# A two-layer diffusion backbone on eight cores: two tiles of the mixing normed ahead, six PSUM banks for its first tile, and a rearranged opening

## The reference

```
for l in range(DEPTH):
    mx = silu(c) @ w_mod[l] + b_mod[l]           # 9 vectors: shift, scale, gate for 3 sub-layers
    h  = h + 0.5 * mx[2] * swiglu(norm_modulate(h, norm_ffn1, mx[0], mx[1]), w_ffn1_in, w_ffn1_out)
    n  = norm_modulate(h, norm_mix, mx[3], mx[4])
    u, q, k, v = split(n @ w_in)                 # 512, 512, 128, 128 columns
    h  = h + mx[5] * concat(pool_mixer(u) @ w_pool * pool_scale, attention(rope(q), rope(k), v)) @ w_out
    h  = h + 0.5 * mx[8] * swiglu(norm_modulate(h, norm_ffn2, mx[6], mx[7]), w_ffn2_in, w_ffn2_out)
return rmsnorm(h, norm_final)
# norm_modulate(x) = x * rsqrt(mean(x^2) + eps) * gain * (1 + scale) + shift;  swiglu: (silu(a) * b) @ w_out
```

## Time and profile before

| | us |
|---|---|
| median of 3 runs | 2917.92 (2917.41 to 2920.98) |
| profiled execution | 2925.55, span 2924.0 on its slowest core (core 0) |
| spans of the 8 cores | 2909.7 to 2924.0, mean granted clock 0.976 to 0.978 |
| busy: PE, DVE, ACT, POOL | 91%, 30%, 27%, 13% |

### The profile page before, as it was taken

The page is one execution under the profiler, slowest core; times in us unless marked ns, Lnnn a source line. Parts: engine busy times, 40 slices in busy tenths (PEclk is TensorE's granted clock), DMA queues, the critical chain, the costliest instruction groups (busy, mean ns, idle before and its releaser), DMA issues.

```text
span 2924.0 us, 46537 instructions; the slowest of 8 cores (2909.7 to 2924.0 us)
## 1 busy us (share of the span) xinstructions
PE 2666.2 (91%) x16692; PEld 1406.1 (48%) x16976; DVE 866.4 (30%) x1568; ACT 798.4 (27%) x1276; POOL 389.3 (13%) x572
## 2 busy tenths in 40 slices
PE   3899999997888799999899999999977888999998
PEld 1455555553444355555455555555534444444445
DVE  2211221214555511132123222222134553112224
ACT  3211321112454511132123112311125453122122
POOL 2111001002322211101100000000023221000000
PEclk9899999998999899999999999999989999999999
DMA  9466356352000165545644341344520003434453
GB/s 212 78 101 107 53 98 103 73 103 48 8 12 6 28 117 97 92 82 87 109 77 79 61 78 32 71 71 78 94 57 8 14 1 66 73 63 88 79 96 130
DMA packets 75706, 214.42 MB, mean 73 GB/s; under 512 B 9184, under 2 KB 17120, under 8 KB 74976
## 3 DMA queue, kind: packets, MB, share of 16 engines
q0 software_dynamic: 60896, 187.33, 37.8%
q1 hardware_dynamic: 14592, 24.12, 2.6%
HBM read 390.32 MB, written 8.39 MB: 136 GB/s over the span
## 4 chain that ended last, share of the span: by engine, by line
PE 85%; issue 4%; DVE 4%; ACT 3%; DMA 3%; POOL 1%; SPq 0%; DVEq 0%; ACTq 0%; POOLq 0%
PE ps L125 74%; PE ps L123 11%; DMA arena<-wab 2%; ACT arena L761 1%; DVE arena L459 1%; ACT arena L468 1%; DMA arena<-gains 1%; DVE arena L663 1%; POOL arena L418 0%; DVE arena L513 0%; SPq L143 0%; DVE arena L788 0%; DVE arena L684 0%; ACT arena L661 0%; ACT arena L429 0%
## 5 line engine op out<-in xcount | busy, mean ns | idle before, releaser
L125 PE MATMUL ps<-arena 128*128 128x512 bf16 (+8 forms) x14581 | 2511.2, 316 | 200.2 <-ACT arena L761 45.6
L125 PEld LDWEIGHTS ps<-arena 128*128 128x128 bf16 (+1 forms) x14829 | 1242.4, 98 | 1290.1 <-issue 274.1
L123 PE MATMUL ps<-arena 128*128 128x512 bf16 (+6 forms) x2111 | 657.0, 335 | 50.8 <-ACT arena L415 26.8
L565 DVE TENSOR_TENSOR arena<-arena,ps 128x512 bf16<-128x512 f32 (+2 forms) x484 | 291.9, 603 | 1184.4 <-PE ps L123 1128.9
L563 ACT ACTIVATE arena<-ps 128x512 f32<-128x512 f32 (+2 forms) x484 | 256.1, 529 | 1183.4 <-PE ps L123 1178.2
L513 DVE SCALAR_TENSOR_TENSOR arena<-ps,arena 128x512 f32<-128x512 f32 (+3 forms) x296 | 177.1, 609 | 569.5 <-PE ps L123 569.3
L123 PEld LDWEIGHTS ps<-arena 128*128 128x128 bf16 (+1 forms) x2147 | 207.2, 99 | 220.9 <-issue 85.6
L468 ACT ACTIVATE arena<-arena 128x512 bf16<-128x512 f32 (+3 forms) x256 | 179.6, 725 | 275.6 <-DVE arena L459 192.8
L143 POOL DMA_DIRECT2D arena<-wab x176 | 94.0, 538 | 645.3 <-PE ps L123 643.5
L761 ACT ACTIVATE arena<-ps 128x1024 bf16<-128x1024 f32 x167 | 161.7, 1027 | 53.3 <-PE ps L123 49.1
L459 DVE TENSOR_TENSOR arena<-arena 128x512 f32<-128x512 f32 (+3 forms) x256 | 156.2, 631 | 26.4 <-ACT arena L431 15.1
(11 more groups left out here) (34 smaller groups left out, 196.2 us busy)
## 6 DMA issues: line engine op xcount, KB each, us to landing
arena<-wab POOLq DMA_DIRECT2D x176, 512.0 KB, 6.5
arena<-wo POOLq DMA_DIRECT2D x64, 704.0 KB, 7.8
arena<-wmod POOLq DMA_DIRECT2D x144, 256.0 KB, 6.5
outT<-arena SPq DMA_DIRECT2D x26, 256.0 KB, 2.4
arena<-xT SPq DMA_DIRECT2D x8, 640.0 KB, 16.5
arena<-xT SPq DMA_DIRECT2D x16, 256.0 KB, 11.0
arena<-wout POOLq DMA_DIRECT2D x4, 1024.0 KB, 10.9
arena<-win POOLq DMA_DIRECT2D x2, 1536.0 KB, 13.1
```

The costliest lines, as they stand in the source:

```text
L123: self.ops["pe"].append(lambda e, l=l, r=r, o_i=o_i, st_i=st_i, sp_i=sp_i: e.matmul(o_i, l, r, start=st_i, stop=sp_i, skip_group_check=sha ...
L125: self.ops["pe"].append(lambda e, l=l, r=r, o_i=o_i, st_i=st_i, sp_i=sp_i: e.matmul(o_i, l, r, start=st_i, stop=sp_i, skip_group_check=sha ...
L565: S.op("dve", lambda e: e.tensor_tensor(gTb[:, j, off:off + n], sa_s[pi][:, 0:n], pb[pi][:, 0:n], ALU.mult), reads=[("sa", pi), BK[2 + pi] ...
```

## The change

`nTt0` is a second normed tile, laid over `pooled` and `aot`, which move down to stand between `wkvu` and `wq`. Tile 0 of the mixing reads it; all other tiles read `nTt`. FFN1's tail norms tile 0 into `nTt0` and tile 1 into `nTt`, so the norm of tile 1 leaves round 0 of the mixing. In round 0 `proj()` takes its banks from six, 6, 7 and 0 to 3. With the new places `wab` slot 0 lies over `pooled`, slot 1 over `aot`, slots 2 and 3 over `wq`, `sa` over `cst`, and the `wm` buffers over `cm` and `band`.

In the opening the loads of bias and gains (`bm`, `gn`) are issued before those of x. A pair of chunks goes to bank c % 4 and no longer to bank 7. The sums of columns 0 to 511 stand after the last in step of the first tile, and their 8 norm steps are spread over the in steps of columns 1024 to 1279.

```diff
         wkvu = alloc(BF16, [8, WKV], dma=True, key=("wkvu",))
+        pooled = parts(BF16, [4, 512], "pooled")
+        aot = parts(BF16, [4, 512], "aot")
+        nTt0 = A.view(pos[0] - 8192, BF16, [8, 512])
+        for k in range(8):
+            S.place(("nTt0", k), pos[0] - 8192 + 1024 * k, 1024)
         wq = alloc(BF16, [8, 512], dma=True, key=("wq",))
         cst = [alloc(F32, [512], dma=True, key=("cs", i)) for i in range(2)]
+        cm = alloc(BF16, [512], dma=True, key=("cm",))
         band = alloc(BF16, [16, BW], dma=True, key=("band",))
-        cm = alloc(BF16, [512], dma=True, key=("cm",))
...
-        pooled = parts(BF16, [4, 512], "pooled")
-        aot = parts(BF16, [4, 512], "aot")
...
+        S.dma("sp", None, bm_l[0], bmod[0], writes=[("bm", 0)])
+        S.dma("sp", None, gn_l[0], gains[0], writes=[("gn", 0)])
         x_load(512, 512)
...
         def mix_tail(l, nmain):
-            norm = norm_steps(0, 512, 1, lambda k, o2, m: nTt[:, k, o2:o2 + m], lambda k: [("nTt", k)], early=True)
+            norms = [norm_steps(0, 512, 1, lambda k, o2, m: nTt0[:, k, o2:o2 + m], lambda k: [("nTt0", k)], early=True),
+                     norm_steps(512, 512, 1, lambda k, o2, m: nTt[:, k, o2:o2 + m], lambda k: [("nTt", k)], early=True)]
             ld = mix_loads(l)
-            return norm_chain([norm]), {nmain // 8: [ld[0]], 3 * nmain // 8: [ld[1]], 5 * nmain // 8: ld[2:]}
+            return norm_chain(norms), {nmain // 8: [ld[0]], 3 * nmain // 8: [ld[1]], 5 * nmain // 8: ld[2:]}
...
+                nTc, nname = (nTt, "nTt") if t else (nTt0, "nTt0")
+                nk = [(nname, k) for k in range(8)]
...
                     ast = a_steps(t)
-                    if t + 1 < 5:
+                    if t == 0:
+                        pbank["l"] = [6, 7, 0, 1, 2, 3]
+                    elif t + 1 < 5:
                         sqs, side = mix_norm(l, t + 1)
...
+        def first_mm(c, chunks):
+            for i, idx in enumerate((c, 8 + c)):
+                key, buf = chunks[idx]
+                S.mm(ps[c % 4][:, 2 * i:2 * i + 2], [(buf[:, k, :], sc[:, k, :]) for k in range(8)],
+                     reads=[key, ("sc",)], writes=[BK[c % 4]])
...
-            late = [(1, {0: norms[2][0], 1: norms[2][1], 2: norms[2][2], 3: norms[0][0]}),
-                    (2, {1: norms[0][1], 2: norms[0][2]}), (0, {})]
+            late = [(1, {0: norms[2][0], 1: norms[2][1], 2: norms[2][2] + norms[0][0], 3: norms[0][1]}),
+                    (2, {0: norms[0][2][0:3], 1: norms[0][2][3:6], 2: norms[0][2][6:8]}), (0, {})]
```

More of the change, by code:

```diff
@@ L622, in mix_norm @@
             n = min(512, (19 if l == DEPTH - 1 else 20) * 128 - t * 512)
-            return norm_steps(512 * t, n, 1, lambda k, o2, m: nTt[:, k, o2:o2 + m], lambda k: [("nTt", k)], eng="dve", bank=6 if t == 0 else 4,
-                              sq="act" if t == 0 else "pool", ahead=t > 0)
+            return norm_steps(512 * t, n, 1, lambda k, o2, m: nTt[:, k, o2:o2 + m], lambda k: [("nTt", k)], bank=4, sq="pool", ahead=True)
         def mix_tail(l, nmain):
             curp["par"] = l % 2
-            norm = norm_steps(0, 512, 1, lambda k, o2, m: nTt[:, k, o2:o2 + m], lambda k: [("nTt", k)], early=True)
+            norms = [norm_steps(0, 512, 1, lambda k, o2, m: nTt0[:, k, o2:o2 + m], lambda k: [("nTt0", k)], early=True),
+                     norm_steps(512, 512, 1, lambda k, o2, m: nTt[:, k, o2:o2 + m], lambda k: [("nTt", k)], early=True)]
             ld = mix_loads(l)
-            return norm_chain([norm]), {nmain // 8: [ld[0]], 3 * nmain // 8: [ld[1]], 5 * nmain // 8: ld[2:]}
+            return norm_chain(norms), {nmain // 8: [ld[0]], 3 * nmain // 8: [ld[1]], 5 * nmain // 8: ld[2:]}
         def mix(l, tail):
@@ L673, in fold @@
                         evac(wf[:, g, 512 * hf:512 * (hf + 1)], p, [pk], [("wf",)])
-            nk = [("nTt", k) for k in range(8)]
             def rope(src, sk, n, o, dst, dkey):
@@ L706, in k_step @@
                     p, pk = proj()
-                    S.mm(p[:, 0:n], [(wkvu[:, k, 512:640], nTt[:, k, 0:n]) for k in range(8)], reads=[("wkvu",)] + nk, writes=[pk])
+                    S.mm(p[:, 0:n], [(wkvu[:, k, 512:640], nTc[:, k, 0:n]) for k in range(8)], reads=[("wkvu",)] + nk, writes=[pk])
                     hold["k"] = rope(p, pk, n, 0, kT[:, c0:c0 + n], ("kT", t))
@@ L713, in v_step @@
                     for tb in range(nb):
-                        pairs += [(nTt[:, k, tb * 128:(tb + 1) * 128], wkvu[:, k, 640:768], p[:, tb * 128:(tb + 1) * 128], k == 0, k == 7) for k in range(8)]
+                        pairs += [(nTc[:, k, tb * 128:(tb + 1) * 128], wkvu[:, k, 640:768], p[:, tb * 128:(tb + 1) * 128], k == 0, k == 7) for k in range(8)]
                     S.mm(p, pairs, reads=[("wkvu",)] + nk, writes=[pk])
@@ L720, in u_step @@
                     p, pk = proj()
-                    S.mm(p, [(nTt[:, k, tb * 128:(tb + 1) * 128], wkvu[:, k, 0:512]) for k in range(8)], reads=[("wkvu",)] + nk, writes=[pk])
+                    S.mm(p, [(nTc[:, k, tb * 128:(tb + 1) * 128], wkvu[:, k, 0:512]) for k in range(8)], reads=[("wkvu",)] + nk, writes=[pk])
                     i = (b0 + tb) % NRING
@@ L729, in q_step @@
                     p, pk = proj()
-                    S.mm(p[:, 0:qn], [(wq[:, k, c * 128:(c + 1) * 128], nTt[:, k, qo:qo + qn]) for k in range(8)], reads=[("wq",)] + nk, writes=[pk])
+                    S.mm(p[:, 0:qn], [(wq[:, k, c * 128:(c + 1) * 128], nTc[:, k, qo:qo + qn]) for k in range(8)], reads=[("wq",)] + nk, writes=[pk])
                     hold[c] = rope(p, pk, qn, qo, qT[t % 3][:, c, qo:qo + qn], ("qT", t % 3, c))
@@ L872, in mix @@
                     pbank["l"] = ([7] if t == 5 else [6, 7]) + [0, 1, 2, 3]
-                    if t + 1 < 5:
+                    if 0 < t < 4:
                         rest = side[9:]
@@ L956, in l0_first @@
         def l0_first():
-            mod_load(0)
             curp["par"] = 0
@@ L965, in l0_first @@
             for c in range(8):
-                for idx in (8 + c, c):
+                for idx in (c, 8 + c):
                     chunks[idx] = mod_load_chunk(0, idx, wide=True)
@@ L971, in l0_first @@
             cnt["ab"] = NWAB
-            x_load(1024, 256, after=[chunks[7][0]])
+            x_load(1024, 256, after=[chunks[15][0]])
             x_load(0, 512, after=[("wab", 1)])
@@ L975, in l0_first @@
             for c in range(8):
-                for idx in (8 + c, c):
-                    mod_mm(idx, *chunks[idx])
+                first_mm(c, chunks)
                 mod_first(c)
                 first[2][c]()
-            late = [(1, {0: norms[2][0], 1: norms[2][1], 2: norms[2][2], 3: norms[0][0]}),
-                    (2, {1: norms[0][1], 2: norms[0][2]}), (0, {})]
+            late = [(1, {0: norms[2][0], 1: norms[2][1], 2: norms[2][2] + norms[0][0], 3: norms[0][1]}),
+                    (2, {0: norms[0][2][0:3], 1: norms[0][2][3:6], 2: norms[0][2][6:8]}), (0, {})]
             extra = mod_tasks(0, [2]) + [lambda: mod_gate(0, 0)] + mod_tasks(0, [4, 3, 5, 7, 6, 8])
```

6 lines of the change are left out of this document (3 added, 3 removed).

## The result

The changed kernel took 2894.5 and 2896.2 us where the kernel before took 2917.4 to 2921.0: ratio 0.992, 95% interval 0.9891 to 0.9949, about 23 us less. The forecast was 2890.

A forecast was written before the change was run, and what follows sets the result against it. TensorE fills 91% of the span, so time comes only from its idle or half-clock stretches: opening 7, rounds 16 and 17.4, less 12.2 for weight loads, 28.2 us off 2917.9, about 2890; 80% range 2880 to 2906.

The forecast's parts named there:

- The likeliest case: Whole kernel: opening and both rounds gain, later weight loads cost, 28.2 us faster in sum, 2890 us; chance 66%.
- the rival in which it eats most: FFN2's first weight load, delayed behind wout, costs 25 us; the change gains only 11, giving 2906 us; chance 14%.
- the norm inside FFN1: FFN1's out steps: the norm moved out of round 0 costs TensorE only its eight sums, 1.8 us per layer.
- The slower rival: FFN2: late weight slots never regain their lead, TensorE waits at each of 88 in steps; costs 44 us, 2934; chance 7%.
- Opening, loads: Start of kernel: bias and gains land early, x's last square 1.0 us later; 1.3 us sooner, 0.6 carried on.
- the start 1 us earlier: Opening: if engines take queues in turn, small loads hardly delay x, starting about 1 us earlier than the forecast took.
- Opening, third tile: Opening, columns 0 to 511: sums and norm moved ahead let TensorE start 6.6 us sooner.
- Round 0: Mixing, both layers: norm moved out and six banks make it shorter by 17.8 and 19.2 us, 16 and 17.4 net.
- Banks that gave nothing: Round 0: read-outs on ACT and DVE bound it, so extra banks give nothing; 7 us less gain, 2897; chance 8%.
- Weight slot: FFN2's first weight load waits for the last wout step: 6.1 and 3.1 us later plus 3.0 half clock, 12.2 cost.
- Fold's chain: Fold in round 0: read-outs alternate on ACT and DVE, each waiting for the one before; 5.9 us for eight.
- the side-by-side case: Fold's eight read-outs run on two engines at once, 2.8 us instead of 5.9; 2884 us; chance 5%.

The follow-up runs named there:

- the kernel with eight keys: Changed kernel with x issued first, `pooled` and `aot` moved above `wq`, and each of `wf`'s eight pieces under its own key: ratio 0.9839 to the kernel before, lowest 2876.04 us.
- both later kernels: Changed kernel with x first, `pooled` and `aot` above `wq`, `wf` under eight keys, without and with split modulation keys: ratios 0.9839 and 0.984 to the kernel before.

## Why the prediction was right, and where it was not

The direction and the time held: 28.2 us were forecast, and the ratio says 23 (15 to 32). The likeliest case is the one that came: the rounds gave 37.3 us and the reload cost 9.2, far from the 25 us of the rival in which it eats most. How close the sum came is luck, though: by the stages the opening gave 6.1 us less than forecast, and the norm inside FFN1 (2.7), the weight loads (3.0) and the rounds (0.3) made up for it. The slower rival (each in step waiting for its slot) is out: beside the two long ones, TensorE's waits for `wab` sum to 8.5 us in 13 (23.8 - 7.85 - 7.44), far from its 44; before they summed to 0.9 to 9.4 us, by core. These terms were off.

- **Opening, loads.** The step that failed is "the last x block's square comes later by up to the two issues' 1.6 us; I take 1.0", hence 1.3 us sooner. The square came 4.0 us later and the first in step 3.4. A late issue was priced by its own length, when it brought x behind the start of the chunk loads. The small loads' own packets are not what holds x: with none ahead of it the late x was as late. "DMA: Bandwidth & Descriptors" of the Trainium skill, "Queues, rings and completion order", says that the engines take their queues in turn by packets. The forecast used this for the small loads, which in the profile share x's own queue; it bears on x against the chunks. There the trace agrees from 6 us on (0.43 MB beside 0.49) and not from 4 to 6 (nothing beside 0.31), and the start 1 us earlier that the forecast drew from it did not come: the squares stand at 10.9 and 29.6 for 5.7 and 25.6. The row had been there: in the earlier trace rows x's blocks were what ACT waited for.
- **Opening, third tile.** 6.6 us forecast, 4.0 to 4.6 measured. From the last sum to the first product the sum had 6.6 us (71.5 to 78.1), with ACT free at 72.7; ACT was held until 76.99, by a SiLU and by blocks whose products DVE made more slowly beside POOL's squares, and it took 7.4. The eight blocks had 12 us and took 13.1, since each in step between them costs 1.5, not 1. Together 1.9 of the 2.0 to 2.6 missing.
- **Round 0.** The sum was right (17.8 and 19.2 forecast, 19.5 and 17.8 measured), its parts were not: banks 6.6 and 7.1 in place of 3.5 a layer, the norm the less. That the two errors cancelled is luck. Banks that gave nothing would have cost 14 us, not the 7 of that rival. The forecast had counted the waits of `a_steps` (3.5, on core 1 they are 3.9), 0.6 for fold's chain where 2.7 came, and left the k step at half clock; with six banks it returned at full clock on four of the eight cores in layer 0 and on two in layer 1. Why the norm gave less in layer 1 than in layer 0 was not looked into.
- **Weight slot.** 12.2 forecast, 9.2 in the table, by the mechanism named: POOL's load late, TensorE's waits 7.9 and 7.4 us, then half clock. The kernel with the slots moved, which takes this cost away and nothing else, says 11.0 (6.4 + 4.6), so the term was better than the table makes it look. The loads took 6.8 and 6.3 us to land, not 7.5 and 5.0.
- **Fold's chain.** The refusal to let the read-outs run side by side was right for this kernel, and the kernel with eight keys shows what the refusal was about. "Perfetto Trace Analysis" of the Trainium skill, "Matmul Optimizations", asks for all eight banks. Here six banks gave 7 us a layer, and the keys, with the same six banks, another 3 (31.4 to 28.4 and 24.0 to 20.8). My 3 us for the side-by-side case hold, but only the keys open it.

## What to carry to other kernels

Moving a load ahead of another one costs the other its place against every queue that starts at the same time, not just the length of the issue: look at what else is issued in that microsecond. When buffers share bytes, the one that is reloaded first should lie over the one whose last reader comes earliest. When a wait is taken away, ask for the next one down (here POOL's squares behind x) before the gain is booked.

## What the runs showed of the hardware

- x issued at 1.51 us, 0.04 before the first of 16 chunk loads, had its first 256 KB squared at 5.7 us (median of the cores); issued at 2.43 or 2.73, 0.9 to 1.2 after it, at 10.9 and 11.1. At the last block the gap is still about 4 us. From 4 to 6 us the queue of the late x moved nothing, the chunks' 0.31 MB; from 6 to 11 they moved 0.43 and 0.49 MB.
- Three DVE products of 128x256 took 2.3 us while POOL squared two blocks of 128x512; before, with POOL idle, two took 0.9 us.
- TensorE's clock was lower where a string of small waits stood ahead. The wait just before fold is the same in all (4.1 to 4.2 us in layer 0). With waits of 0.3 to 0.6 us in fold and the pooling behind it, seven matmuls of the k step took 2.48 to 3.15 us on the eight cores (3.15 is 1.2 GHz throughout). With fold's eight matmuls in one run they took 1.67 (2.4 GHz) on four of eight cores in the changed kernel, but on one of eight in the kernel with the slots moved. With the read-outs side by side they took 1.67 to 1.73 on all eight in both later kernels; in layer 1 there, 1.67 to 2.56.
